# Router coefficients split into two DRAM tensors by token half, with the expert choice reordered and packed into 30 down tiles

## What is computed

```python
def peer_ffn(h, w_query, sub_keys1, sub_keys2, expert_down, expert_up):
    q = (h @ w_query).reshape(B, S, PEER_HEADS, 2, HALF_KEY)
    s1 = jnp.einsum('bshd,nd->bshn', q[..., 0, :], sub_keys1).astype(jnp.float32)
    s2 = jnp.einsum('bshd,nd->bshn', q[..., 1, :], sub_keys2).astype(jnp.float32)
    v1, i1 = lax.top_k(s1, TOPK_HALF)
    v2, i2 = lax.top_k(s2, TOPK_HALF)
    cand = (v1[..., :, None] + v2[..., None, :]).reshape(B, S, PEER_HEADS, TOPK_HALF * TOPK_HALF)
    cand_idx = (i1[..., :, None] * N_KEYS + i2[..., None, :]).reshape(...)
    top_v, pos = lax.top_k(cand, TOPK)
    expert_idx = jnp.take_along_axis(cand_idx, pos, axis=-1)
    gates = jax.nn.softmax(top_v, axis=-1).astype(h.dtype)
    ...
        u = jnp.take(expert_down, idx_blk, axis=0)
        act = jax.nn.gelu(jnp.einsum('bpd,bphkd->bphk', h_blk, u))
        vv = jnp.take(expert_up, idx_blk, axis=0)
        return jnp.einsum('bphk,bphkd->bpd', g_blk * act, vv)
```

## Time and profile before

| | us |
|---|---|
| device time, median of 3 runs (1553.6 to 1555.4) | 1553.85 |
| span of the profiled execution, first to last instruction | 1550.4 |
| PE busy, 10099 matmuls | 1510.6 (97%) |
| DVE busy | 1013.9 (65%) |
| ACT busy | 663.4 (43%) |
| POOL busy | 425.8 (27%) |

### The profile page before, as it was taken

One profiled execution on the slowest core, in us unless ns is written; L12 is line 12 of the kernel. 1 busy time (PEld: TensorE's weight loads), 2 busy tenths in 40 slices (PEclk: granted clock), 3 DMA queues, 4 the chain that ended last, 5 costly groups with the idle time before them and its releaser, 6 DMA issues.

```text
span 1550.4 us, 25630 instructions
## 1 busy us (share of the span) xinstructions
PE 1510.6 (97%) x10099; PEld 1280.4 (83%) x10099; DVE 1013.9 (65%) x1829; ACT 663.4 (43%) x1009; POOL 425.8 (27%) x285
## 2 busy tenths in 40 slices
PE   8999999999999888999999999999999999999998
PEld 6777878875655575799999999999999888888887
DVE  5888787755765755678998733333334777777776
ACT  4455453633322511434434443434344444454553
POOL 0000000000011200018888888888882000000000
PEclk9999999999999999999999999999999999999999
DMA  9776664448655902446665656666663777777776
GB/s 342 268 261 226 209 239 137 162 163 258 227 207 175 407 19 67 160 147 178 137 150 137 148 139 148 140 144 143 146 142 95 239 239 242 240 238 238 239 239 231
DMA packets 166075, 297.25 MB, mean 192 GB/s; under 512 B 49539, under 2 KB 70323, under 8 KB 165957
## 3 DMA queue, kind: packets, MB, share of 16 engines
q1 hardware_dynamic: 119680, 277.08, 53.0%
q0 software_dynamic: 39296, 8.55, 7.6%
q10 hardware_dynamic: 6980, 9.99, 2.1%
HBM read 276.54 MB, written 19.03 MB: 191 GB/s over the span
## 4 chain that ended last, share of the span: by engine, by line
PE 91%; DVE 4%; issue 2%; ACT 1%; DMA 1%; SPq 0%; DVEq 0%
PE bank L553 23%; PE bank L555 22%; PE bank L557 22%; PE bank L1166 7%; PE bank L548 6%; PE bank L1097 1%; PE bank L1113 1%; PE bank L903 1%; PE bank L915 1%; PE bank L605 1%; PE bank L526 1%; PE bank L914 1%; DVE gt L1273 1%; PE bank L1157 0%; PE bank L598 0%
## 5 line engine op out<-in xcount | busy, mean ns | idle before, releaser
L2591 POOL DMA_INDIRECT c_dram<-gates,places x256 | 403.3, 1575 | 165.1 <-DVE gates L1962 87.5
L1292 DVE TENSOR_TENSOR dT_low<-bank,dT_high 128x512 fp32r<-128x512 f32 x256 | 165.0, 687 | 217.5 <-ACT dT_high L2488 150.6
L553 PE MATMUL bank<-hT_high,dT_high 128*128 128x256 f32 x1024 | 298.9, 292 | 0.1
L555 PE MATMUL bank<-hT_low,dT_high 128*128 128x256 f32 x1024 | 288.1, 281 | 0.0
L557 PE MATMUL bank<-hT_high,dT_low 128*128 128x256 f32 x1024 | 284.7, 278 | 0.0
L2500 ACT CAST up_high<-slot 128x1024 fp32r<-128x1024 f32 x128 | 134.5, 1051 | 160.1 <-DMA slot<-in_expert_up_dram 160.1
L553 PE MATMUL bank<-up_high,A_high 128*128 128x512 f32 x512 | 200.0, 391 | 1.2 <-DVE A_low L1292 1.2
L555 PE MATMUL bank<-up_low,A_high 128*128 128x512 f32 x512 | 200.7, 392 | 0.0
L557 PE MATMUL bank<-up_high,A_low 128*128 128x512 f32 x512 | 199.2, 389 | 0.0
L557 PEld LDWEIGHTS bank<-hT_high,dT_low 128*128 128x128 f32 x1024 | 193.4, 189 | 0.0
L553 PEld LDWEIGHTS bank<-hT_high,dT_high 128*128 128x128 f32 x1024 | 192.8, 188 | 0.3 <-issue 0.3
(11 more groups left out here) (449 smaller groups left out, 2370.5 us busy)
## 6 DMA issues: line engine op xcount, KB each, us to landing
slot<-in_expert_down_dram SPq DMA_DIRECT2D x128, 512.0 KB
slot<-in_expert_up_dram SPq DMA_DIRECT2D x128, 512.0 KB, 3.6
slot<-in_w_in_dram SPq DMA_DIRECT2D x41, 1024.0 KB, 5.4
P<-in_w_ada_dram SPq DMA_DIRECT2D x16, 1024.0 KB, 7.7
c_dram<-zeros SPq DMA_DIRECT2D x1, 16384.0 KB, 51.0
slot<-c_dram SPq DMA_DIRECT2D x128, 128.0 KB, 3.5
slot<-in_w_in_dram SPq DMA_DIRECT2D x6, 2048.0 KB, 8.4
slot<-in_w_out_dram SPq DMA_DIRECT2D x8, 1024.0 KB, 5.2
```

What stands on the lines that cost most here:

```text
L553: pe.matmul(o, lhsT=lhs_high.bitcast(F32R), rhs=rhs_high.bitcast(F32R), start=start, stop=False, skip_group_check=True)
L555: pe.matmul(o, lhsT=lhs_high.bitcast(F32R), rhs=rhs.bitcast(F32R), start=False, stop=False, skip_group_check=True)
L1292: return v.tensor_tensor(dst.bitcast(F32R), src, high, ALU.subtract)
L2591: g.indirect_dma_start(C_dram, bass.IndirectOffsetOnAxis(ap=places[:, x, k:k + 1], axis=0), gates[:, x, k:k + 1], None, compute_op=ALU.add ...
```

## The change

It has three parts. The coefficient tensor becomes two, one for each half of the tokens, so the zeroing and the load of a tile's coefficients are two DMAs each of half the size, and the load's rows are 512 bytes. POOL scatters the first half's heads one after the other, with two of the 16 scatters of head 0 of the second half after each of them, and then heads 1 to 7 of the second half, one after the other. And the choice goes in the order of `PICKS`, each entry with its own `v_picks`: after the two entries of pair 0, the first halves of pairs 1 to 3 and then their second halves, in two parts ahead of each of the down tiles 0 to 29. ACT's exponentials follow, one for each entry (six instead of three among the down tiles).

```diff
-    C_dram = nc.dram_tensor("c_dram", [N_KEYS * N_KEYS * S, 1], F32, kind="Internal").ap()
+    C_dram = [nc.dram_tensor(f"c_dram{t}", [N_KEYS * N_KEYS * P, 1], F32, kind="Internal").ap() for t in range(TT)]
+    PICKS = [(0, 0), (0, 1), (1, 0), (2, 0), (3, 0), (1, 1), (2, 1), (3, 1)]
...
-    def v_picks(c, part, ts=range(TT)):
-        n, rows = PAIRS * len(ts), slice(PAIRS * ts.start, PAIRS * ts.stop)
+    def v_picks(c, t, part):
+        rows, at = slice(PAIRS * t, PAIRS * (t + 1)), TP * c + PAIRS * t
...
-        for c in range(1, 4):
-            for t in range(TT):
-                for part in range(5):
-                    v_top(c, t, part)
-                    v_tile_turn(15 * (c - 1) + 5 * t + part)
-            for part in range(5):
-                v_picks(c, part)
-                v_tile_turn(15 * (c - 1) + 10 + part)
-        for n in range(45, N_KEYS):
+        for n, (c, t) in enumerate(PICKS[2:]):
+            for half in range(5):
+                for part in (2 * half, 2 * half + 1):
+                    if part < 5:
+                        v_top(c, t, part)
+                    else:
+                        v_picks(c, t, part - 5)
+                v_tile_turn(5 * n + half)
+        for n in range(30, N_KEYS):
             v_tile_turn(n)
...
-            if n in (10, 25, 40):
-                a_gates(1 + n // 15)
+            if n % 5 == 1 and n < 30:
+                a_gates(*PICKS[2 + n // 5])
...
+    def g_head_here(h, t):
+        if h % PAIRS == 0:
+            g.wait_ge(picks_ready, 2 * (PICKS.index((h // PAIRS, t)) + 1))
+        if h:
+            g.wait_ge(scattered[t][(h - 1) % 2], 16 * TOPK * ((h - 1) // 2 + 1))
+
     def g_experts():
...
+        for h in range(PEER_H):
+            g_head_here(h, 0)
+            for k in range(TOPK):
+                g_scatter(h, 0, k)
+            if h == 0:
+                g_head_here(0, 1)
+            for k in range(2 * h, 2 * h + 2):
+                g_scatter(0, 1, k)
+        for h in range(1, PEER_H):
+            g_head_here(h, 1)
+            for k in range(TOPK):
+                g_scatter(h, 1, k)
...
     def s_coeff(p):
         if p > 3:
             sp.wait_ge(gated, p - 3)
-        sp.dma_start(coeff[p % 4], C_dram[p * P * S:(p + 1) * P * S].rearrange("(e n) o -> e (n o)", n=S)
-                     ).then_inc(coeff_in[p % 4], 16)
+        for t in range(TT):
+            sp.dma_start(coeff[p % 4][:, t * P:(t + 1) * P],
+                         C_dram[t][p * P * P:(p + 1) * P * P].rearrange("(e n) o -> e (n o)", n=P)).then_inc(coeff_in[p % 4], 16)
```

More of the change, by code:

```diff
@@ L1930, in v_keys @@
                                      key_of[:, x, rows].unsqueeze(2).broadcast_to([P, n, TOPK, TOPK]), ALU.mult))
-    def v_picks(c, part, ts=range(TT)):
-        n, rows = PAIRS * len(ts), slice(PAIRS * ts.start, PAIRS * ts.stop)
-        g4 = gates[:, TP * c + rows.start:TP * c + rows.stop, :]
+    def v_picks(c, t, part):
+        rows, at = slice(PAIRS * t, PAIRS * (t + 1)), TP * c + PAIRS * t
+        g4 = gates[:, at:at + PAIRS, :]
         if part == 0:
-            v.tensor_tensor(g4, top_v[:, rows], top_v[:, rows, 0:1].broadcast_to([P, n, TOPK]), ALU.subtract).then_inc(gate_shifted, 1)
+            v.tensor_tensor(g4, top_v[:, rows], top_v[:, rows, 0:1].broadcast_to([P, PAIRS, TOPK]), ALU.subtract).then_inc(gate_shifted, 1)
             v.tensor_scalar(rank_u[:, 0, rows], top_at[:, rows], 4, None, ALU.logical_shift_right)
@@ L1943, in v_picks @@
         elif part == 1:
-            v_match(0, rows, n)
-            v_keys(0, rows, n)
+            v_match(0, rows, PAIRS)
+            v_keys(0, rows, PAIRS)
         elif part == 2:
             v.tensor_reduce(sel_key[:, 0, rows], eq[0][:, rows], AX, ALU.add)
-            v_match(1, rows, n)
+            v_match(1, rows, PAIRS)
         elif part == 3:
-            v_keys(1, rows, n)
+            v_keys(1, rows, PAIRS)
             v_own.settle(v.tensor_reduce(sel_key[:, 1, rows], eq[1][:, rows], AX, ALU.add))
@@ L1954, in v_picks @@
                                                 ALU.mult, ALU.add))
[L1955 to L1959, removed]
+            v.tensor_scalar(places[:, at:at + PAIRS, :], rank[:, 0, rows, :], float(P), tokens[:, 0:1],
+                            ALU.mult, ALU.add).then_inc(picks_ready, 1)
+            v.wait_ge(gate_exp, PICKS.index((c, t)) + 1)
             v_own.settle(v.tensor_reduce(gate_norm[:, rows], g4, AX, ALU.add))
             v_own.settle(v.reciprocal(gate_norm[:, rows], gate_norm[:, rows]))
-            v.tensor_tensor(g4, g4, gate_norm[:, rows].unsqueeze(2).broadcast_to([P, n, TOPK]), ALU.mult).then_inc(picks_ready, 1)
+            v.tensor_tensor(g4, g4, gate_norm[:, rows].unsqueeze(2).broadcast_to([P, PAIRS, TOPK]), ALU.mult).then_inc(picks_ready, 1)
     def v_tile_turn(n):
@@ L1973, in v_choose @@
             v_top(0, 0, part)
-        v_picks(0, 0, range(1))
-        v_picks(0, 1, range(1))
+        v_picks(0, 0, 0)
+        v_picks(0, 0, 1)
         v_query_split(0)
-        v_picks(0, 2, range(1))
-        v_picks(0, 3, range(1))
+        v_picks(0, 0, 2)
+        v_picks(0, 0, 3)
         v_query_split(1)
-        v_picks(0, 4, range(1))
+        v_picks(0, 0, 4)
         for part in range(3):
@@ L1987, in v_choose @@
         for part in range(5):
-            v_picks(0, part, range(1, 2))
-        for c in range(1, 4):
-            for t in range(TT):
-                for part in range(5):
-                    v_top(c, t, part)
-                    v_tile_turn(15 * (c - 1) + 5 * t + part)
-            for part in range(5):
-                v_picks(c, part)
-                v_tile_turn(15 * (c - 1) + 10 + part)
-        for n in range(45, N_KEYS):
+            v_picks(0, 1, part)
+        for n, (c, t) in enumerate(PICKS[2:]):
[7 more added lines that the diff above has]
+        for n in range(30, N_KEYS):
             v_tile_turn(n)
@@ L2001, in v_gate @@
         clear(v, ("down", p))
-        v.wait_ge(coeff_in[p % 4], 16 * (p // 4 + 1))
+        v.wait_ge(coeff_in[p % 4], 32 * (p // 4 + 1))
         v.tensor_tensor(G[:, p, :], G[:, p, :], coeff[p % 4], ALU.mult).then_inc(gated, 1)
@@ L2458, in a_query @@
         a_query_split(1)
-        a_gates(0, range(1))
+        a_gates(0, 0)
         for t in range(2):
@@ L2469, in a_query @@
             a_score_copy(2, t)
-        a_gates(0, range(1, 2))
+        a_gates(0, 1)
         for t in range(2):
@@ L2474, in a_query, with a_gates @@
             a_score_copy(3, t)
[L2476 to L2479, removed]
+    def a_gates(c, t):
+        a.wait_ge(gate_shifted, PICKS.index((c, t)) + 1)
+        x = gates[:, TP * c + PAIRS * t:TP * c + PAIRS * (t + 1), :]
         a.activation(x, x, ACT.Exp).then_inc(gate_exp, 1)
@@ L2515, in a_experts @@
             if n == KEPT:
-                a.wait_ge(picks_ready, 13)
+                a.wait_ge(picks_ready, 16)
             if n == N_KEYS - 1:
@@ L2578, in g_rwkv, with g_scatter @@
         g.tensor_tensor(by_head(v_), by_head(v_), each(bonus_h), ALU.mult).then_inc(bonus_v, 1)
-    def g_experts():
[L2581 to L2592, removed]
+    def g_scatter(h, t, k):
+        x = TP * (h // PAIRS) + PAIRS * t + h % PAIRS
+        g.indirect_dma_start(C_dram[t], bass.IndirectOffsetOnAxis(ap=places[:, x, k:k + 1], axis=0),
+                             gates[:, x, k:k + 1], None, compute_op=ALU.add).then_inc(scattered[t][h % 2], 16)
+    def g_head_here(h, t):
[3 more added lines that the diff above has]
+            g.wait_ge(scattered[t][(h - 1) % 2], 16 * TOPK * ((h - 1) // 2 + 1))
+    def g_experts():
+        g.wait_ge(zeroed, 32)
+        for h in range(PEER_H):
[10 more added lines that the diff above has]
+                g_scatter(h, 1, k)
     g_late()
@@ L2658, in s_chunks @@
                 sp.wait_ge(zeros_set, 1)
-                sp.dma_start(C_dram.rearrange("(p a b) o -> p a (b o)", p=P, b=CW),
-                             zeros.unsqueeze(1).broadcast_to([P, N_KEYS * S // CW, CW])).then_inc(zeroed, 16)
+                for t in range(TT):
+                    sp.dma_start(C_dram[t].rearrange("(p a b) o -> p a (b o)", p=P, b=CW),
+                                 zeros.unsqueeze(1).broadcast_to([P, N_KEYS * P // CW, CW])).then_inc(zeroed, 16)
     def s_tail():
```

## The result

| | before | changed |
|---|---|---|
| device time, median (4 runs each), us | 1554.62 (1553.6 to 1555.75) | 1581.29 (1578.89 to 1585.63) |
| ratio, 95% interval | | 1.0172 [1.0152, 1.0192] |
| span of the profiled execution, us | 1550.4 | 1577.6 |
| PE busy, us (10099 matmuls in both) | 1510.6 | 1521.0 |

The forecast was 1579.2, with a range of 1574 to 1587.

A forecast was written before the change was run, and what follows sets the result against it. PE bounds the kernel before; after the change DVE's pace does among the first 30 down tiles. 24.9 us there plus 0.5 for the coefficient loads, 25.4 onto 1553.85, gives 1579.2 us, range 1574 to 1587.

The forecast's parts named there:

- The step that carried the sum: First 30 down tiles: two choice parts plus `dT_low` cost DVE 22.96 us per five tiles, 4.59 each against PE's 3.70.
- The walk: Follows DVE's `dT_low` starts from tile 0 to tile 29, whose products begin at 854.3 instead of 829.39: 24.9 us late.
- DVE's pieces: Start-to-start times of the choice's parts and `dT_low` among the down tiles, given 3% either way, 4 us of 137.8.
- the coefficient loads: Up tiles: two half loads instead of one, the second mostly hidden; 0.5 us in all, 5 us as upper end.
- Rival 1: PE's clock falls among the first 30 down tiles: some 1.7 us at 0.83, total 1600 at 0.70; chance 0.06.
- The landings: POOL waits seven times for a landing in the second half's scatters, 13.6 us in all, hidden behind the later down tiles.
- Rivals 2 to 4: Up tiles bound by coefficients (1592, chance 0.06); landings take longer (1590, 0.03); DVE's pieces fit, PE never waits (1553.9, 0.04).
- No scatter waits for the choice: Reading of POOL's 256 scatters before the change: they don't wait for the choice, so finishing it earlier sets nothing free.

The follow-up runs named there:

- the lighter choice: Changed kernel without parts 1 and 2 of `v_top` for the last six entries, still two parts a tile in the same 30 tiles: 1565.27 us.
- the half-packed run: Changed kernel with two parts a tile for three of the last six entries (15 tiles), one part for the other three (30 tiles): 1567.31 us.
- the smoother cut: Changed kernel with the same ten parts of the choice in five tiles cut 2, 1, 1, 3, 3 instead of two each: 1582.97 us.

## Why the prediction was right

**The step that carried the sum held.** Five tiles of DVE were worked out at 22.96 us; in the trace after, `dT_low` of tile 0 starts at 720.64 and that of tile 25 at 835.97, 23.07 for five. The walk put PE 24.9 us late at tile 29. Counted from the start of `dT_low` of tile 0 (0.86 us later than before, for reasons ahead of the change), the shift is 27.16 - 0.86 = 26.3. The 1.4 beyond the forecast are 0.5 from DVE's pieces (854.15 - 720.64 = 133.51 against 132.98) and, the rest, from PE's clock: tile 29's products begin 856.55 - 854.15 = 2.40 after its `dT_low`, where tile 0 of the kernel before needed 1.43 and I had added 0.15. The run with the old scatter order bears that out: from 840.4 to 862 its granted clock was 1.00, and its tile 29 began 858.72 - 857.13 = 1.59 after its `dT_low`. A little luck is in the sum too: the 0.5 that I had put on the coefficient loads didn't come and made up for part of the 1.4.

**Rival 1 came true in its mild form.** The granted clock was 0.95 in the stage, where I had priced 0.83 at 1.7 us; it cost about 0.8 at tile 29. What I had wrong was the picture, not the sum: I expected some 25 us of waits of PE. The trace has 16.4 of them, and PE is busy 10.4 us longer with the same 10099 matmuls (1521.0 against 1510.6). Slow products fill part of the holes that DVE leaves, so they mostly cost nothing. The rule on bursts and waits that I quoted from the Trainium skill ("TensorE: Matmul & The Clock Gate", "HAM oscillation") is borne out in part. The clock did fall among bursts and waits. But of the five tiles behind waits of 2.5 to 2.6 us only one, tile 21 (from 820.93), started low; 6 and 26 started high and fell within the tile, and 11 and 16 stayed high.

**The landings were mis-sized, and hidden.** I took 2.24 us for each from the one landing in the earlier trace rows, 13.6 us in all after taking off the 0.30 between scatters. Seven waits were 20.3 us, 2.9 each, and up to 3.9. From the first start to the last the scatters took 1191.9 - 693.7 = 498.2 us, 18.8 more than in the earlier trace rows. The down tiles ended 27 us later, so nothing of it shows. The two runs in which they did not end so late, with one part a tile and with the lighter choice, show the price: 5.8 and 3.9 us of idle PE ahead of the up tiles, and 1.8 and 2.5 of clock behind it. The first half's heads, with two scatters between them, waited for nothing, as forecast (in the half-packed run one of them did, 0.70 us).

**The coefficient loads cost nothing** instead of my 0.5: from the first up product to the end the trace after takes 1577.6 - 1220.85 = 356.7 us, as before. The loads of 64 KB landed in 3.1 us (median) where those of 128 KB took 3.5, and the second is issued about 0.5 us behind the first, so the second half lands some 0.1 later; the "some 1 us" that I allowed at worst shows in no run. The DMA share of 0.77 isn't their doing alone: with only the two tensors it stayed at 0.74.

**Rivals 2 to 4** didn't come true; the pieces did not fit, and their sum was within 0.5% of what the rows said.

**One reading was too broad.** "No scatter waits for the choice" holds from the second scatter on. The first one waits 87.5 us for the `gates` of pair 0, before and after. That part of the choice lies ahead of the down tiles and the change leaves it as it was, so nothing in the sum hangs on it.

## What to carry to other kernels

When work is moved closer together on an engine that isn't the bound, divide its new demand for each step by the bound's pace in the same stage: 4.59 against 3.70 us a tile was the whole result, and it was to be read from start-to-start times before anything was built. Look also at who needs the work early: here the choice of the later pairs was ready long before the scatters wanted it, and PE, not the scatters, set the end, so to hurry it could win nothing. And an order that takes away the work between two dependent transfers shows its landing times, hidden or not: the 5.5 us of the scatter order would have come up as soon as the first fault was mended.

## What the runs showed of the hardware

After equal waits PE's clock did not always do the same. In the changed kernel five tiles follow a wait of 2.5 to 2.6 us: 6 and 26 slow down within the tile, 21 is slow from its first product (granted clock 0.52 from 820.90 to 824.40), 11 and 16 keep the higher level. In the smoother cut, where no wait for `dT_low` was over 2.02 us, the clock still fell in three of the five tiles behind the longest waits. Behind the waits of 5.84 and 3.92 us the up tiles began at the lower level (0.50). Among the down tiles the effect on the time was small because DVE was the bound; among the up tiles, where PE is, it was 1.8 and 2.5 us.

Two large DMAs behind each other on SP's queue can hold the queue. This is the timeline of SP at the zeroing, in the trace after:

```profile
495.66 20.85 SPq L2670 DMA_DIRECT2D c_dram<-zeros  x2
```

The one zeroing of 16 MB had been issued in 0.61 us; of the two of 8 MB the second kept SP for 20.2 us. Nothing was late for it, since SP's next wait for PE shrank by as much (its longest from 118.3 to 98.2 us). SP takes its queue in order, so a load queued behind it would have gone out later; no run put one there.
